# Encoder trunk in fp32 on one core: output projection reordered by row tiles, two-pass norm, and layer 2's token low parts from PSUM

## The chip, the core and the metric

One core of a Trainium2 chip runs the whole program. Times are device microseconds from the first to the last instruction of the core, as the runs give them. Engines: TensorE (PE, with its weight loads PEld), VectorE (DVE), ScalarE (ACT), GpSimd (POOL), SyncE (SP), which issues all the DMAs.

## What is computed

Two encoder layers over x (1, 1024, 1024), with D_MODEL = 1024 and D_INNER = 2048. Layer i does

```python
q, k, v, mq, gate = split_proj(einsum('bld,de->ble', x, w_in[i]), SPLIT)
o_mix = mixer_a(...) if i == 0 else mixer_b(...)     # windowed / dilated attention, 12 heads
o_mem = memory_attention(mq, mem, w_mkv[i])          # 4 heads
y = concat([o_mix, o_mem]) * silu(gate)              # (1024, 2048)
branch = einsum('ble,ed->bld', y, w_out[i])          # 2048 -> 1024
x = layer_norm(ALPHA * x + branch, ln_g[i], ln_b[i])
```

Everything is fp32. Below, *the first layer* is layer 0 of the code and *the second layer* its layer 1.

## The kernel before

**Products in three parts.** TensorE multiplies fp32r operands. Each fp32 operand is split in two, by ScalarE (`split_hi`, `columns_hi`, `y_tile`: a copy that rounds to fp32r, the high part) and VectorE (`split_lo`, `columns_lo`: the source less the high part, the low part). A product is three matmuls: high by high, high by low, low by high. Weights come by DMA in pieces of 128x512 (256 KB) into `raw` (6 slots), and are split into `ring` (4 slots, each a high and a low part); `AHEAD = 3` is how many pieces ahead the splits are issued.

**Input projection (`run`).** Each layer is a row of *pairs* of 128-column blocks (20 in the first layer, 40 in the second). A pair is computed from 7 products of 4 steps of 3 matmuls each (a Strassen-like scheme, 84 matmuls of 512 columns), with 7 operands made of the tokens, `xs[j]`, j = 0 to 6. Operand j is a half of the rows, or a sum or difference of halves (`token_sums` and its sisters, VectorE). Its rows have tokens on the partitions, and TensorE transposes them, four 128x128 blocks to a *group* (`x_group`, `rows_to_columns`, line 1063), into one of the four banks XB; ScalarE's copy (line 1306) takes the high part and VectorE's subtraction (lines 1581, 1536) the low part. There are 28 groups to a layer. `X_BEFORE` says ahead of which product of the first pair TensorE transposes which operands; in the second layer it is operand 0 before product 0, operands 1 and 2 before product 1, 3 before 2, 4 before 3, and 5 and 6 before product 4. The attention of earlier pairs is interleaved with the steps.

**Output projection (`out_projection`).** y comes back from DRAM in tiles of 128x512 (`y_raw`, two slots) and is split too (`y_split`, two slots). For each half h of the tokens and each block e of the 16 of D_INNER, TensorE adds 24 matmuls into all eight PSUM banks (4 token tiles by 2 column halves; `add_to`, lines 1256, 1260, 1262). All eight banks of a half end in its last two blocks (`last_two`). So the sums of the rows come at the end of a half, nearly together:

```python
for h in range(2):
    for e in range(NE - 2):
        is_split(h, e)
        for b in range(8):
            add_to(h, e, b, first=e == 0, ends=b >= 6)
    last_two(h)
```

VectorE then adds the residual (`add`, line 1878), and takes mean and variance (`statistics`, lines 1886 and 1889). GpSimd makes the standard deviation's inverse (`norms`: add epsilon, power -1/2, for tiles 4 to 7 two more for the bias). Rows 0 to 3 are normalised beside the second half's matmuls: VectorE subtracts the mean and multiplies (line 1896), multiplies by g, and GpSimd adds b over 128x1024 (line 1044). For rows 4 to 7, ScalarE normalises (line 1521), and VectorE multiplies by g and adds b (lines 1901 and 1904), each a `scalar_tensor_tensor` over 128x1024 by the helper `two`, line 1536. Its loop for the norms stands after the adds and statistics of all four tiles, so all the norms follow the last statistics.

**Order.** Each engine runs its own list; they meet in semaphores. SP's list holds the loads of weights (`loads_after`, released by `w_lo`), of y, the residual rows, g and b, the stores of y, and, after all the loads of the projection, the stores of the normalised rows (lines 997 and 1000). In the second layer TensorE takes operand 0 from rows 0 to 3 as soon as banks 4 to 7 are free; ScalarE reaches those groups after its four norms; VectorE reaches operand 0's low parts after its eight multiplications and additions. The first pair's `first_part` on ScalarE waits for all eight rows (lines 1324, 1325), because it writes into the same buffer.

## Time and profile before

| | |
|---|---|
| runs | 2168.25, 2169.8, 2172.13 us; median 2169.8 |
| profiled execution | 2170.46 us, of which the span is 2168.6 us |
| TensorE busy | 2107.2 us, 97% |
| VectorE busy | 1628.4 us, 75% |
| ScalarE busy | 1091.1 us, 50% |
| mean granted clock | 0.990 |

A row of the timeline gives the start and the time from the first start to the last end of one or more instructions. Matmuls overlap: one of 512 columns is listed with 0.39 us, but in a run of them a new one begins every 0.227 us at the full clock. The granted clock is 1.00 for 2.4 GHz and 0.50 for 1.2 GHz. "issue" is time in which the engine waited for nothing that the profile shows.

### The profile page before, as it was taken

How to read it: one execution, taken by the hardware profiler on the slowest of the kernel's cores; microseconds unless marked ns; L12 is line 12 of the kernel's file. 1: busy time of each engine (PE TensorE's matmuls, PEld its weight loads, DVE VectorE, ACT ScalarE, POOL GpSimd, SP SyncE). 2: the span in 40 equal slices, each digit the busy share in tenths (PEclk: the TensorE clock that was granted, in tenths of full speed). 3: DMA queues.
4: the chain of work that ended last, by engine and by line, in shares of the span. 5: the costliest groups of instructions: out<-in, count | busy, mean ns of one | idle time of the engine just before them, and what ended most of it. 6: DMA issues, size and time to landing. Idle time of an engine off the chain costs nothing.

```text
span 2168.6 us, 31853 instructions
## 1 busy us (share of the span) xinstructions
PE 2107.2 (97%) x10880; PEld 1767.9 (82%) x10880; DVE 1628.4 (75%) x3673; ACT 1091.1 (50%) x2649; POOL 48.4 (2%) x65
## 2 busy tenths in 40 slices
PE   8999999999999995999999999999999999999996
PEld 8888888888888774888888888888888888888875
DVE  6777878787663568868888888888887888775485
ACT  5444444445553323455555555555555565564332
POOL 0000000000000021000000000000000000000031
PEclk9999999999999997999999999999999999999998
DMA  8311111111126542123233133133143233224643
GB/s 266 103 48 42 60 39 49 59 59 59 54 80 216 182 141 102 54 69 94 63 97 93 56 100 95 50 108 99 50 108 86 63 108 85 89 87 161 216 142 131
DMA packets 244619, 209.20 MB, mean 96 GB/s; under 512 B 21092, under 2 KB 198316, under 8 KB 244460
## 3 DMA queue, kind: packets, MB, share of 16 engines
q1 hardware_dynamic: 244460, 207.16, 31.8%
q8 instruction: 89, 1.46, 0.3%
q14 instruction: 70, 0.57, 0.1%
HBM read 172.60 MB, written 34.52 MB: 96 GB/s over the span
## 4 chain that ended last, share of the span: by engine, by line
PE 78%; DVE 13%; DMA 5%; issue 2%; ACT 2%; SPq 0%; DVEq 0%; ACTq 0%
PE bank L1086 15%; PE bank L1084 15%; PE bank L1085 15%; PE bank L1162 8%; PE bank L1134 7%; DVE work L1536 5%; PE bank L1256 4%; PE bank L1260 4%; PE bank L1262 4%; PE bank L1148 4%; DVE ring L1536 2%; DMA work<-weight_scratch 1%; DMA weight_scratch<-trig 1%; DVE x_ops L1536 1%; PE bank L1063 1%
## 5 line engine op out<-in xcount | busy, mean ns | idle before, releaser
L1084 PE MATMUL bank<-x_ops,ring 128*128 128x512 f32 (+1 forms) x1808 | 844.5, 467 | 16.9 <-issue 14.8
L1086 PE MATMUL bank<-x_ops,ring 128*128 128x512 f32 (+1 forms) x1808 | 698.9, 387 | 0.0
L1085 PE MATMUL bank<-x_ops,ring 128*128 128x512 f32 (+1 forms) x1808 | 697.0, 386 | 0.0
L1536 DVE SCALAR_TENSOR_TENSOR ring<-raw,ring 128x512 fp32r<-128x512 f32 x400 | 272.9, 684 | 232.9 <-ACT ring L1302 232.6
L1086 PEld LDWEIGHTS bank<-x_ops,ring 128*128 128x128 f32 x1808 | 341.0, 189 | 71.3
L1084 PEld LDWEIGHTS bank<-x_ops,ring 128*128 128x128 f32 x1808 | 345.7, 191 | 61.4 <-issue 15.5
L1363 ACT COPY work<-bank 128x256 f32<-128x256 f32 (+2 forms) x448 | 164.3, 367 | 430.1 <-PE bank L1148 429.3
L1085 PEld LDWEIGHTS bank<-x_ops,ring 128*128 128x128 f32 x1808 | 345.5, 191 | 37.5
L1302 ACT CAST ring<-raw 128x512 fp32r<-128x512 f32 x400 | 246.5, 618 | 198.4 <-PE bank L1262 173.0
L1162 PEld LDWEIGHTS bank<-work 128*128 128x128 f32 x1744 | 262.2, 190 | 44.4 <-ACT work L1363 3.9
L1380 ACT ACTIVATE work<-work,soft 128x256 f32<-128x256 f32 (+2 forms) x448 | 226.5, 506 | 134.3 <-DVE soft L1680 132.6
L1134 PE MATMUL bank<-work 128*128 128x256 f32 (+2 forms) x896 | 267.2, 380 | 3.0 <-DVE soft L1680 3.0
L1162 PE MATMUL bank<-work 128*128 128x128 f32 x1744 | 267.6, 275 | 2.5 <-ACT work L1363 1.2
L1536 DVE SCALAR_TENSOR_TENSOR work<-work 128x512 f32<-128x512 f32 (+4 forms) x352 | 233.3, 678 | 34.5 <-DMA work<-weight_scratch 31.5
L1134 PEld LDWEIGHTS bank<-work 128*128 128x128 f32 x896 | 183.3, 215 | 39.9 <-DVE soft L1680 7.8
L1536 DVE SCALAR_TENSOR_TENSOR work<-work,trig 32x512 f32<-32x512 f32 x304 | 207.2, 710 | 0.8
L1256 PE MATMUL bank<-ring,x_ops 128*128 128x512 f32 x512 | 200.4, 391 | 6.9 <-DVE x_ops L1536 5.3
L1262 PE MATMUL bank<-ring,x_ops 128*128 128x512 f32 x512 | 199.3, 389 | 0.0
L1260 PE MATMUL bank<-ring,x_ops 128*128 128x512 f32 x512 | 199.3, 389 | 0.0
L1536 DVE SCALAR_TENSOR_TENSOR ring<-sums,ring 128x512 fp32r<-128x512 f32 x180 | 123.0, 683 | 68.2 <-ACT ring L1302 68.1
L1148 PE MATMUL bank<-ident,work 128*128 128x128 f32 x872 | 168.7, 273 | 0.5 <-DVE work L1690 0.5
L1148 PEld LDWEIGHTS bank<-ident,work 128*128 128x128 f32 x872 | 114.2, 140 | 34.9 <-ACT work L1380 4.5
(74 smaller groups left out, 2020.8 us busy)
## 6 DMA issues: line engine op xcount, KB each, us to landing
raw<-in_w_in_b SPq DMA_DIRECT2D x160, 256.0 KB, 3.1
raw<-in_w_out SPq DMA_DIRECT2D x128, 256.0 KB, 2.9
raw<-in_w_in_a SPq DMA_DIRECT2D x80, 256.0 KB, 3.0
work<-weight_scratch SPq DMA_DIRECT2D x24, 768.0 KB, 5.2
y_scratch<-work SPq DMA_DIRECT2D x32, 512.0 KB, 2.8
x_ops<-y_scratch SPq DMA_DIRECT2D x64, 256.0 KB, 3.7
work<-v_scratch SPq DMA_DIRECT2D x48, 256.0 KB, 4.4
raw<-in_w_mkv SPq DMA_DIRECT2D x32, 256.0 KB, 5.1
```

The source lines that it names most:

```text
L1084: nc.tensor.matmul(dst, w_h, x_h, start=start, stop=False, skip_group_check=again)
L1085: nc.tensor.matmul(dst, w_h, x_l, start=False, stop=False, skip_group_check=again)
L1086: return nc.tensor.matmul(dst, w_l, x_h, start=False, stop=stop, skip_group_check=again)
L1134: nc.tensor.matmul(SB[count % 2][:, 0:size], q, k, start=True, stop=True).then_inc(s_ready, 1)
L1148: mm = nc.tensor.transpose(TB[x_n % 2][:, c * P:(c + 1) * P], p[:, k0:k0 + P], ident[:, :])
L1162: mm = nc.tensor.matmul(dst, job.values(v), pT[layer][count % 2][:, c * P:(c + 1) * P], start=(c == 0), stop=(c == len(chunks) - 1))
L1256: mm = nc.tensor.matmul(BB[b][:, :], y_h, ring[:, n % RING, 0, :], start=first, stop=False)
L1260: nc.tensor.matmul(BB[b][:, :], y_h, ring[:, n % RING, 1, :], start=False, stop=False)
L1262: mm = nc.tensor.matmul(BB[b][:, :], y_l, ring[:, n % RING, 0, :], start=False, stop=last)
L1302: nc.scalar.copy(ring[:, n % RING, 0, :], src).then_inc(w_hi, 1)
L1380: nc.scalar.activation(p_view(layer, count % 3, size, sink), s_view(layer, count % 3, size, sink), ACT.Exp, bias=low[:, job.stat, t:t + 1] ...
L1536: return nc.vector.scalar_tensor_tensor(out=dst, in0=a, scalar=1.0, in1=b, op0=ALU.mult, op1=op)
```

## The change

**Output projection.** The 16 blocks fall into twelve early ones and four late ones (8 to 11). In each half, TensorE does the early blocks over all eight banks as before, and then, for one bank after the other, the four late blocks: 12 matmuls to a bank, so that a token tile is done every 24 matmuls. The late blocks' split weights are kept for both halves (`late`, 8 places in the region of operands 4 and 5, split once a layer, in the first half); their split y has four places of its own. So a layer's projection has 56 weight pieces and not 64. `y_raw` gets four slots. `AHEAD` is 3 as before, but the calls count single pieces.

**Norm.** VectorE adds epsilon; GpSimd's share is the power alone. VectorE does (x - mean) * g in one `scalar_tensor_tensor` (`scale`) and (that * rstd) + b in another (`shift`), both over 128x1024; for every tile of the second half both follow the tile's own statistics. ScalarE's norm, GpSimd's additions of b and VectorE's separate passes go. In the second layer the last tile is shifted and stored in two halves of the columns.

**Second layer's operands.** Operand 0's groups and their low parts are done within the first layer's output projection, three groups after token tile 6 (the third of the second half), one after tile 7. For operands 0 to 5 the low part is made in PSUM: a matmul of minus the unit matrix by the high part is added to the transposed group (`less_high`), and ScalarE copies the rest (`x_low`). Operand 5 moves to product 1, so that twelve groups (5, 1, 2) precede it. VectorE keeps the low parts of operand 6 alone. The token sums of the first kinds move from the second layer's beginning into the norm loop.

```diff
-OUT_STAGES = 4 * NE
+EARLY = (0, 1, 2, 3, 4, 5, 6, 7, 12, 13, 14, 15)
+LATE = (8, 9, 10, 11)
...
-RAW, RING, AHEAD = 6, 4, 3
+RAW, RING, AHEAD, Y_RAW = 6, 4, 3, 4
...
-                    ((0,), (1, 2), (3,), (4,), (5, 6), (), ()))
+                    ((), (5, 1, 2), (3,), (4,), (6,), (), ()))
...
+            def deviations(layer):
+
+                for t in range(TILES):
+                    pool.wait_ge(ln_eps, layer * TILES + t + 1)
+                    nc.gpsimd.tensor_tensor(rstd[:, t:t + 1], mv[:, t, 1:2], power[:, 0:1],
+                                            ALU.pow).then_inc(ln_rstd, 1)
...
+            def less_high(j, i):
+
+                number = x_number(1, j, i)
+                pe.wait_ge(xt_hi, number + 1)
+                nc.tensor.matmul(x_bank(number)[:, :].rearrange("p (k n) -> p k n", k=4), minus,
+                                 xs[:, j, 0, :, i * P:(i + 1) * P], start=False, stop=True,
+                                 skip_group_check=True).then_inc(xt_less, 1)
...
-                    if j == 0 and layer == 1:
-                        pe.wait_ge(z_free, 16)
+                    if j < 2 and layer == 1:
+                        pe.wait_ge(z_free, 8 + BRANCH_BANKS.index(j) + 1)
...
                 for h in range(2):
-                    for e in range(NE - 2):
+                    for e in EARLY:
                         is_split(h, e)
                         for b in range(8):
-                            add_to(h, e, b, first=e == 0, ends=b >= 6)
-                    last_two(h)
+                            add_to(h, e, b, first=e == EARLY[0], ends=b >= 6)
+                    for t in range(4):
+                        for c in range(2):
+                            for e in LATE:
+                                if t == 0 and c == 0:
+                                    is_split(h, e)
+                                add_to(h, e, 2 * t + c, last=e == LATE[-1])
+                        if layer == 0 and h == 1 and t >= 2:
+                            for i in ((0, 1, 2), (3,))[t - 2]:
+                                x_group(1, 0, i)
+                            for i in ((0, 1), (2, 3))[t - 2]:
+                                less_high(0, i)
...
+            def x_low(j, i):
+                number = x_number(1, j, i)
+                act.wait_ge(xt_less, number - 4 - X_GROUPS + 1)
+                nc.scalar.copy(xs[:, j, 1, :, i * P:(i + 1) * P],
+                               x_bank(number)[:, :].rearrange("p (k n) -> p k n", k=4)
+                               ).then_inc(xt_rest, 1)
...
+                second = 2 * NE + AHEAD
+                for m in range(AHEAD, second):
+                    stage(m)
+                for t in range(4):
+                    add(0, 2 * t)
+                    add(0, 2 * t + 1)
+                    statistics(t)
+                for m in range(second, OUT_STAGES + AHEAD):
+                    stage(m)
+                    t, step = divmod(m - second - 8, 2)
+                    if 0 <= t < 4:
+                        if step == 0:
+                            scale(t)
+                        else:
+                            shift(t, slice(0, D), ln_done)
+                if layer == 0:
                     third_sum(FIRST_PAIR[1])
                     fourth_sum(FIRST_PAIR[1])
                 for t in range(4, TILES):
-                    norm(t)
+                    add(1, 2 * (t - 4))
+                    add(1, 2 * (t - 4) + 1)
+                    statistics(t)
+                    if layer == 0 and t > 4:
+                        token_sums(1, t - 5)
+                        second_token_sums(1, t - 5)
+                    scale(t)
+                    if layer == 1 and t == 7:
+                        for half in HALVES:
+                            shift(t, half, ln_done_v)
+                    else:
+                        shift(t, slice(0, D), ln_done_v)
+                if layer == 0:
+                    token_sums(1, 3)
+                    second_token_sums(1, 3)
```

In `run(1)`, TensorE and ScalarE take the groups of a product one behind the other: group n is transposed (its high part copied), then `less_high` (and `x_low`) of group n - 1.

## Rows read from the trace of the kernel before

**Rows 1.** The page: busy time of each engine, and the chain by engine.
```profile
PE 2107.2 (97%) x10880; PEld 1767.9 (82%) x10880; DVE 1628.4 (75%) x3673; ACT 1091.1 (50%) x2649; POOL 48.4 (2%) x65
...
PE 78%; DVE 13%; DMA 5%; issue 2%; ACT 2%; SPq 0%; DVEq 0%; ACTq 0%
```

**Rows 2.** Busy time, granted clock and DMA by stretch; columns in line one.
```profile
core 0: us, PE busy (x) PEld busy (x) DVE busy (x) ACT busy (x) POOL busy (x), PEclk, DMA share, GB/s
...
646.40:736.00 89.60, 87.98 (x387) 72.48 (x388) 37.42 (x57) 29.98 (x50) 0.00 (x0) 1.00 0.64 209
736.00:825.70 89.70, 87.90 (x383) 71.06 (x381) 56.98 (x77) 27.55 (x46) 16.64 (x12) 1.00 0.49 159
825.70:849.00 23.30, 3.65 (x16) 2.70 (x16) 22.92 (x34) 7.93 (x10) 6.52 (x16) 0.58 0.22 90
849.00:854.00 5.00, 4.97 (x13) 3.89 (x14) 4.86 (x8) 0.00 (x0) 0.00 (x0) 0.55 0.00 0
854.00:861.00 7.00, 4.23 (x32) 3.49 (x31) 7.00 (x13) 4.31 (x9) 0.00 (x0) 0.95 0.00 0
...
870.00:887.00 17.00, 16.82 (x97) 14.07 (x96) 14.39 (x25) 9.14 (x18) 0.00 (x0) 1.00 0.12 32
```

**Rows 3.** Timeline of TensorE between the layers and through pair 20.
```profile
825.27 0.39 PE L1262 MATMUL bank<-ring,x_ops 128*128 128x512 f32 x1
...
849.03 0.76 PE L1084 MATMUL bank<-x_ops,ring 128*128 128x512 f32 x1 [14.82 <-issue]
...
874.18 1.91 PE L1063 MATMUL bank<-ident,work 128*128 128x128 f32 x16
...
886.48 0.39 PE L1086 MATMUL bank<-x_ops,ring 128*128 128x512 f32 x1
```

**Rows 4.** Timeline of VectorE between the layers.
```profile
832.38 1.24 DVE L1878 SCALAR_TENSOR_TENSOR work<-work,bank 128x512 f32<-128x512 f32 x2
833.66 1.29 DVE L1886 BATCH_NORM_STATS2 work<-work 128x6 f32<-128x512 f32 x2
834.98 0.21 DVE L1889 BATCH_NORM_AGGREGATE work<-work 128x2 f32<-128x12 f32 x1
...
836.86 9.67 DVE L1536 SCALAR_TENSOR_TENSOR work<-work 128x1024 f32<-128x1024 f32 x8
846.46 2.48 DVE L1536 SCALAR_TENSOR_TENSOR x_ops<-bank,x_ops 128x512 fp32r<-128x512 f32 x4
```

**Rows 5.** Timeline of TensorE at the end: its last matmul.
```profile
2150.66 0.39 PE L1262 MATMUL bank<-ring,x_ops 128*128 128x512 f32 x1
```

**Rows 6.** Timeline of VectorE at the end: its last group.
```profile
2155.98 9.62 DVE L1536 SCALAR_TENSOR_TENSOR work<-work 128x1024 f32<-128x1024 f32 x8
```

**Rows 7.** Waits of TensorE, 646 to 826 us: us in total, times, longest.
```profile
PE bank L1256 <- DVE x_ops L1536: 3.3, 5, 1.6
```

**Rows 8.** Waits of TensorE, 2063 to 2151 us: the same columns.
```profile
PE bank L1256 <- DVE x_ops L1536: 1.7, 4, 0.9
```

**Rows 9.** Timeline around 784 us: start us, us, engine, line, operation.
```profile
783.82 2.77 POOL L1044 TENSOR_TENSOR work<-work 128x1024 f32<-128x1024 f32 x1 [3.24 <-DVE work L1536]
...
784.26 2.88 DVE L1536 SCALAR_TENSOR_TENSOR x_ops<-x_ops 128x512 fp32r<-128x512 f32 x1
```

**Rows 10.** Timeline of ScalarE: copies of transposed columns in PSUM.
```profile
874.82 4.50 ACT L1306 CAST x_ops<-bank 128x512 fp32r<-128x512 f32 x8 [1.88 <-PE bank L1063]
```

**Rows 11.** Timeline of GpSimd: the power -1/2, VectorE light and busy.
```profile
2148.25 0.55 POOL L1032 TENSOR_TENSOR work<-work,power 128x1 f32<-128x1 f32 x1
...
2157.29 1.54 POOL L1032 TENSOR_TENSOR work<-work,power 128x1 f32<-128x1 f32 x1
```

**Rows 12.** DMA queue and issues, 646 to 736 us (KB each, us to landing).
```profile
GB/s 124 242 312 236 255 11 249 94 147 203 32 254 272 245 238 223 267 213 247 276 201 261 203 258 279 203 303 180 230 297 214 233 264 263 306 267 113 0 45 72
...
raw<-in_w_out SPq DMA_DIRECT2D x31, 256.0 KB, 3.1
x_ops<-y_scratch SPq DMA_DIRECT2D x16, 256.0 KB, 4.4
```

More of the change, by code:

```diff
@@ L60 @@
 MKV_STAGES = 4 * DEPTH * MEM_HEADS
-OUT_STAGES = 4 * NE
+EARLY = (0, 1, 2, 3, 4, 5, 6, 7, 12, 13, 14, 15)
+LATE = (8, 9, 10, 11)
+OUT_ORDER = []
+for half in range(2):
+    for place, block in enumerate(EARLY):
+        OUT_ORDER += [(half, block, 0), (half, block, 1)]
+        if half == 0 and place % 3 == 1:
+            OUT_ORDER += [(0, LATE[place // 3], 0), (0, LATE[place // 3], 1)]
+OUT_STAGES = len(OUT_ORDER)
+Y_ORDER = [(half, block) for half in range(2) for place, early in enumerate(EARLY)
+           for block in ((early, LATE[place // 3]) if place % 3 == 1 else (early,))]
 LAYER_STAGE = (MKV_STAGES, MKV_STAGES + PRODUCTS * PAIRS[0] + OUT_STAGES)
@@ L341, in encoder @@
         weight_in = sem("weight_in")
-        y_full = [sem("y_full0"), sem("y_full1")]
+        y_full = [sem(f"y_full{b}") for b in range(Y_RAW)]
         y_hi = sem("y_hi")
@@ new lines, in load_norm @@
+            def load_norm(layer, place):
+                row, src = ((g_row, ln_g), (b_row, ln_b))[place]
+                nc.sync.dma_start(row, src[layer].partition_broadcast(P)).then_inc(gb_in, 16)
+                if layer == 0 and place == 1:
+                    for m, src in ((m_b, mask_b), (m_w, mask_w), (m_b2, mask_b2)):
+                        nc.sync.dma_start(m, src).then_inc(mask_in, 16)
+            def out_projection(layer, residual, dst):
+                for m in range(AHEAD, OUT_STAGES + AHEAD):
+                    loads_after(OUT_STAGE[layer] + m)
+                    if m >= OUT_STAGES:
+                        continue
+                    h, e, c = OUT_ORDER[m]
+                    if c == 1 and e in EARLY:
+                        place = EARLY.index(e)
+                        if h == 0 and 5 <= place < 9:
+                            load_residual(layer, residual, place - 5)
+                        if h == 0 and place >= 10:
+                            load_norm(layer, place - 10)
+                        if h == 1 and 1 <= place < 5:
+                            load_residual(layer, residual, 3 + place)
+                    for q in y_events(m):
+                        if q + Y_RAW - 1 < 2 * NE:
+                            load_y(layer, q + Y_RAW - 1)
@@ L1182, in run @@
                             if g == FIRST_PAIR[layer]:
-                                for op in X_BEFORE[layer][j]:
-                                    for i in range(4):
-                                        x_group(layer, op, i)
+                                groups = [(op, i) for op in X_BEFORE[layer][j] for i in range(4)]
+                                for n, group in enumerate(groups):
+                                    x_group(layer, *group)
+                                    if layer == 1 and j < 4 and n > 0:
+                                        less_high(*groups[n - 1])
+                                if layer == 1 and j < 4 and groups:
+                                    less_high(*groups[-1])
                             product_begins(g, j)
@@ L1455, in run @@
                     if T < STEPS and T % 4 == 0:
-                        for op in X_BEFORE[layer][T // 4]:
-                            for i in range(4):
-                                x_group(layer, op, i)
+                        groups = [(op, i) for op in X_BEFORE[layer][T // 4] for i in range(4)]
+                        for n, group in enumerate(groups):
+                            x_group(layer, *group)
+                            if layer == 1 and T < 16 and n > 0:
+                                x_low(*groups[n - 1])
+                        if layer == 1 and T < 16 and groups:
+                            x_low(*groups[-1])
                     if T in fills[layer]:
@@ L1786, in run @@
                     if T < STEPS and T % 4 == 0:
+                        for op in X_BEFORE[layer][T // 4] if layer == 0 or T == 16 else ():
+                            for i in range(4):
+                                x_group(layer, op, i)
                         if layer == 1 and T in (4, 8):
@@ new lines, in scale @@
+                def scale(t):
+                    n = layer * TILES + t
+                    dve.wait_ge(ln_aggr, n + 1)
+                    dve.wait_ge(gb_in, 32 * (layer + 1))
+                    nc.vector.scalar_tensor_tensor(out=rows[:, t, :], in0=rows[:, t, :],
+                                                   scalar=mv[:, t, 0:1], in1=g_row,
+                                                   op0=ALU.subtract, op1=ALU.mult
+                                                   ).then_inc(ln_scaled, 1)
@@ new lines, in shift @@
+                def shift(t, cols, done):
+                    n = layer * TILES + t
+                    dve.wait_ge(ln_scaled, n + 1)
+                    dve.wait_ge(ln_rstd, n + 1)
+                    nc.vector.scalar_tensor_tensor(out=rows[:, t, cols], in0=rows[:, t, cols],
+                                                   scalar=rstd[:, t:t + 1], in1=b_row[:, cols],
+                                                   op0=ALU.mult, op1=ALU.add).then_inc(done, 1)
+                second = 2 * NE + AHEAD
```

341 lines of the change are left out of this document (144 added, 197 removed).

## The prediction

> **What bounds the kernel now.** I read the page first, for who is busy and who ends the chain: TensorE is busy 97% of the span and holds 78% of the chain, VectorE 13% [rows 1]. So only the places where TensorE stands still can give anything. The busy time by stretch shows where they are [rows 2]: both halves of the first layer's output projection are nearly full, and then come 23.3 us in which TensorE works for 3.65 us and VectorE for 22.92. The timeline gives the edges [rows 3]: the last matmul of the projection is issued at 825.27 and is through its slot at 825.5; the second layer's first product begins at 849.03; its first pair (pair 20) ends with the matmul of 886.48, at 886.7. That is 61.2 us for 84 matmuls that need 19.0 at 0.227 each. In between stands VectorE's list [rows 4]: per token tile two additions, two statistics and one aggregate (2.72 us from tile to tile), then eight passes of 1.2 us over 128x1024 (836.86 to 846.5), and only then operand 0's low parts (846.46, four of them), which release the product at 849.03. The end of the program has the same shape: last matmul at 2150.66, so done with its slot at 2150.9 [rows 5], VectorE's eight passes until 2165.6 [rows 6], last store landed at 2168.6, 3.0 us later. Last, TensorE's waits in the projections: 3.3 us [rows 7] and 1.7 us [rows 8] for the low parts of y. They have a cause: beside a 2.77 us addition of b on GpSimd, VectorE's low part of y takes 2.88 us, where its neighbours take 0.69 [rows 9].
>
> **Part 1, the projection.** It keeps 768 matmuls a layer; the order by tile changes their sequence, not their number. Twelve of them in a row into one bank is what the products of a pair do already, so I price that at nothing. GpSimd's four long additions a layer go, and with them the 5.0 us of waits [rows 7, 8]. What takes their place on VectorE, in the second half's early blocks, is per block two weight splits, one y split (0.6 each) and two passes of 1.2: 4.2 us, 4.8 in a block that also splits a late y, under the 5.44 us of its 24 matmuls. In the first half the late pieces make VectorE's and ScalarE's work per early block four thirds of before, about 2.4 us; that is covered as well. Between the halves VectorE's adds and statistics now come tile by tile; after the last bank it has about 2.7 us of them and 1.3 us of splits before the second block of the new half is needed, 5.44 us later: 1.4 us of cover, nothing charged. GpSimd's small operations and SP's order cost nothing: residual rows are asked for some 20 us ahead or more, the y tiles three ahead. **Gain 5.0 us**; bounds 0 (if other waits come) and 6.
>
> **Part 2, between the layers.** Time is counted from the last projection matmul, P.
> - Inserted before P: twelve transposes (16 take 1.91 us [rows 3], so 1.4) and two minus products of 0.23 with a short wait: 2.0 us on TensorE, which move no other thing.
> - After P: one group, its high copy, the last minus products, the last low copies by ScalarE (0.56 us each, from eight in 4.50 [rows 10]): 2.4 us. Product 0, 12 matmuls: 2.7. So it ends at P+5.1, where it now begins only at P+23.5 [rows 3].
> - ScalarE's first copy out of product 0 waits for the last tile's `shift`. VectorE works tile by tile: 2.72 for adds and statistics, 0.15 for epsilon (the aggregate takes 0.21 [rows 4]), 1.2 scale, some 0.35 waiting for GpSimd, 1.2 shift, and 1.2 of token sums: 6.8 us a tile against 5.44 plus the inserted groups. After P the last tile needs about 0.6 (latency, second addition) + 1.5 + 0.15 + 1.2 of token sums + 1.2 + 1.2: P+6.0. The copy of 0.7 ends at P+6.7. It is TensorE's queue behind `less_high` that waits, since the groups of product 1 stand ahead of product 1.
> - The twelve groups of product 1 need 24 copies on ScalarE, where now it makes one per group and VectorE the other side by side. 24 x 0.56 = 13.5 us if TensorE keeps its clock. TensorE then has per group 0.43 of transposes and 0.23 of product in 1.12 us. In the trace, the stretch of 7 us with only transposes and a gap behind product 0 ends at the lower level (0.95 over 854 to 861 [rows 2], and 0.58 in the gap before, where TensorE stood), while 4.3 us of transposes behind product 3 do not (1.00 over 870 to 887). A stretch of 13 us is nearer to the first. So I take the lower clock from about 4 us after product 0: ten groups at 4 x 0.213 + 0.43 = 1.3 us, 1.8 more than ScalarE's pace, plus what is in flight: the groups end at P+22.5. Product 1 then runs mostly at 1.2 GHz as 849 to 854 does (0.55 [rows 2]): 4.9 us and not 2.7: P+27.4.
> - Products 2 and 3: each is preceded by a copy of 0.7 and eight copies, 4.5 us, then 2.7: 7.9 each, P+43.2. VectorE did half of those copies before; now it is free there, which is worth nothing.
> - Operand 6 (1.9, VectorE makes the low part) and products 4 to 6 (8.2): P+53.3.
> In all 53.3 + 2.0 = 55.3 against 61.2: **gain 5.9 us**. With the full clock throughout it is 48.8 + 2.0, a gain of 10.4. The lower bound: the clock falls again in the groups of products 2, 3 and 4 (rival 2), a loss of 2.
>
> The cost of a minus product is not in the trace. Between nothing (hidden under the copies) and a whole slot at the low clock, 24 x 0.43 = 10 us, I take what the copies leave, because ScalarE's pace is the longer one.
>
> **Part 3, the end.** Now 2168.6 - 2150.9 = 17.7 us. After: VectorE needs 2.72 + 0.15 + 1.2 + 0.35 + 1.2 = 5.6 us a tile against TensorE's 5.44, so it is 0.6 late at the last tile and 0.2 behind by the matmul's latency. Then the second addition 0.65, statistics 1.5, epsilon 0.15, scale 1.2, waiting for the power 0.35, two half shifts 1.2, and the half tile's store: 2.9, from the 256 KB loads at 3.1 [rows 12] and today's 3.0 for 512 KB. Sum 8.7: **gain 9.0 us**. Bounds 7 and 10.5. The power takes 0.55 us on GpSimd with VectorE light and 1.54 beside the 128x1024 passes [rows 11]; 0.35 is what 1.54 leaves beyond the 1.2 of scale. The Trainium skill, "SBUF — State Buffer", "SBUF: two separate sides", says that a VectorE operation with two SBUF inputs and a GpSimd operation that reads SBUF exclude each other for a whole instruction. By that rule the power begins only when scale is over, each wait is some 0.65, and VectorE falls 1.2 us further behind at the end; the doubled times of [rows 9] agree with it.
>
> **Sum.** 5.0 + 5.9 + 9.0 = 19.9 us off the profiled execution of 2170.46 gives 2150.6. The median of the runs is 0.7 below that execution; so 2150.
>
> **Rivals.**
> 1. *The clock stays up* between the layers, because the gaps between pieces of work are under a microsecond. For: 4.3 us of transposes at 1.00 [rows 2]. Against: 13 us are three times that. 2170.5 - 5.0 - 10.4 - 9.0 = 2146.1, by the median 2145.
> 2. *The clock comes back for moments only.* Transposes don't keep it up, so it falls in the groups of products 2, 3 and 4 as well, since only 2.7 us of product lie between them. Each of two stretches costs 4 x 0.18 more for its groups and 2.4 for its product, 3.1; operand 6 and product 4 cost 1.7: 7.9 in all, 2158. Against it: 1.00 over 870 to 887 with two such stretches. The Trainium skill, "TensorE: Matmul & The Clock Gate", "PE-mode transpose", says that transposes don't count as busy in the way matmuls do. By that rule this rival is the case; the full clock behind 4 us of transposes [rows 2] neither proves nor refutes it.
> 3. *The chain of a group is serial*: high copy, minus product, low copy with the semaphores between, 1.5 us and not 1.12, because ScalarE's list alternates and finds the product unready. 20 groups x 0.38 = 7.6 later than with full clock or 5 later than forecast: 2155 to 2160.
> 4. *Slower: the loads bind the early blocks of the first half.* All 32 weight pieces, 16 y tiles, 4 residual rows, g and b, 16 MB, must now come in 65 us: 246 GB/s, where the trace shows 209 over the stretch at 0.64 share [rows 2]. If they came at 200, the early blocks would take 80 us, 14.7 more in each layer, 29.4 together: 2150 + 29 = 2179. It decides from about 217 GB/s downwards (10 us a layer eats the gain). Against it: single slices run at 250 to 312 GB/s [rows 12], pieces land in 3.1 and 4.4 us with six and three in flight, and 0.64 of the share for 209 leaves room for 320.
> 5. *The change does less than it says*: the pipeline by tile holds, but VectorE's order (token sums ahead of scale) delays the last shift by more than counted. It only moves ScalarE's gate, some 2 us: within the range.
>
> **How the numbers follow.** The forecast gets 0.45, rival 1 gets 0.25, rival 2 gets 0.13, rival 3 gets 0.08, rival 4 gets 0.04; 0.05 stays for a better outcome than all, a lower price of tail and gate together. The range goes from 2142 (rival 1 with the better ends of parts 1 and 3) to 2160 (rivals 2 and 3). A measurement of this kernel can tell about 0.2%, 4.3 us, from no change. Faster by more than that: all but rival 4 and a little of 2 and 3 with part 1 at its bound of nothing: 0.93. Within it 0.03, slower 0.04.
>
> **What would show it.** Waits of TensorE for low parts of y near zero in both projections; a gap under 3 us between the last projection matmul and product 0; TensorE at 60 to 80% with ScalarE at its copies in the next 15 us, and the granted clock there (0.5 or 1.00 tells the forecast from rival 1); pair 20 over some 53 us after P; VectorE one tile behind TensorE at the end, and the last store landing 8 to 9 us after the last matmul. I am wrong if TensorE waits for splits in the early blocks of a first half, if VectorE is more than a tile late, or if the twelve groups take over 18 us.

## The result, and the profile after

The changed kernel takes 2141.39 us (median of 4 runs, 2140.49 to 2143.5) against 2169.03 (4 runs, 2168.05 to 2172.13): ratio 0.9872, 95% interval 0.9854 to 0.9889. The forecast was 2150 (2142 to 2160): the direction was right, the size was not: 27.6 us were gained where the forecast had some 20. A second measurement (F1) gave 2143.4 us, ratio 0.9868 (0.9854 to 0.9882). The profiled execution has a span of 2138.7 us.

The page of the changed kernel, the rows that answer to [rows 1], and TensorE's costliest groups:

```profile
PE 2108.1 (99%) x10904; PEld 1771.9 (83%) x10904; DVE 1592.9 (74%) x3650; ACT 1078.2 (50%) x2650; POOL 16.6 (1%) x23
...
PE 85%; DVE 6%; DMA 3%; ACT 2%; issue 2%; SPq 1%; POOL 0%; DVEq 0%; POOLq 0%; ACTq 0%
...
L1157 PE MATMUL bank<-x_ops,ring 128*128 128x512 f32 (+1 forms) x1808 | 842.8, 466 | 2.8 <-DVE ring L1622 2.1
...
L1331 PE MATMUL bank<-ring,x_ops 128*128 128x512 f32 x384 | 149.6, 390 | 1.5 <-issue 1.5
```

TensorE's busy time is the same within 1 us; its share of the chain rises from 78% to 85%, VectorE's falls from 13% to 6%. `add_to` over the early blocks (the last row) waits for VectorE nowhere.

Where the time came from is best read by milestones of TensorE, in us from one to the next. They are worked out from the timelines of the two kernels (a matmul's slot of 0.227 is added to the last of a stage):

| stage | before | after | gain | forecast |
|---|---|---|---|---|
| start to the first projection | 646.45 | 645.88 | 0.6 | 0 |
| first projection, without the inserted 2.0 us | 179.05 | 174.35 | 4.7 | 3.3 |
| inserted groups and products | 0 | 2.0 | -2.0 | -2.0 |
| last projection matmul to product 0 | 23.5 | 2.5 | 21.0 | 21.1 |
| product 0 to the end of pair 20 | 37.7 | 45.0 | -7.3 | -13.2 |
| the other 39 pairs | 1086.2 | 1084.8 | 1.4 | 0 |
| second projection | 177.95 | 174.2 | 3.75 | 1.7 |
| last matmul to the end | 17.7 | 9.9 | 7.8 | 9.0 |

The sum is 29.9 us of span, where the forecast's terms sum to 19.9. "The other 39 pairs" took 1084.8 to 1092.0 us in the profiled executions of ten kernels that have the same code there, so 1.4 can't be put down to the change.

Busy time, granted clock and DMA by stretch, for [rows 2]:

```profile
core 0: us, PE busy (x) PEld busy (x) DVE busy (x) ACT busy (x) POOL busy (x), PEclk, DMA share, GB/s
646.40:729.00 82.60, 82.60 (x366) 68.38 (x365) 41.21 (x67) 29.11 (x51) 1.11 (x2) 1.00 0.64 208
729.00:822.25 93.25, 93.25 (x417) 77.06 (x416) 59.39 (x89) 24.46 (x43) 4.91 (x5) 1.00 0.44 150
...
827.60:831.10 3.50, 1.02 (x9) 0.78 (x7) 3.32 (x4) 1.15 (x4) 0.00 (x0) 0.98 0.12 48
831.10:834.70 3.60, 3.56 (x15) 3.01 (x15) 3.60 (x7) 2.73 (x6) 0.00 (x0) 0.55 0.26 101
834.70:842.90 8.20, 7.45 (x40) 4.90 (x38) 0.31 (x1) 8.20 (x17) 0.00 (x0) 1.00 0.00 0
842.90:858.00 15.10, 13.39 (x69) 10.18 (x68) 3.79 (x6) 11.25 (x23) 0.00 (x0) 1.00 0.18 53
```

Both projections are full. The clock did fall between the layers, but for less than 4 us (0.55 over 831.1 to 834.7), behind a stretch in which TensorE had worked 1.02 of 3.5 us. It came back within the groups, and stayed.

TensorE's timeline there, for [rows 3]. Line 1127 is the transposes, 1151 the minus product, 1331 to 1333 the projection, 1157 to 1159 the products of a pair:

```profile
822.02 0.39 PE L1333 MATMUL bank<-x_ops 128*128 128x512 f32 x1
...
824.75 0.47 PE L1157 MATMUL bank<-x_ops,ring 128*128 128x512 f32 x1 [0.72 <-issue]
...
827.58 1.03 PE L1127 MATMUL bank<-ident,work 128*128 128x128 f32 x8
831.14 0.80 PE L1151 MATMUL bank<-x_ops 128*128 128x512 f32 x1 [2.52 <-ACT x_ops L1376]
...
832.44 0.78 PE L1151 MATMUL bank<-x_ops 128*128 128x512 f32 x1
...
835.72 0.51 PE L1151 MATMUL bank<-x_ops 128*128 128x512 f32 x1
...
836.70 0.50 PE L1151 MATMUL bank<-x_ops 128*128 128x512 f32 x1
...
842.58 0.50 PE L1151 MATMUL bank<-x_ops 128*128 128x512 f32 x1 [0.48 <-ACT x_ops L1376]
842.92 0.40 PE L1157 MATMUL bank<-x_ops,ring 128*128 128x512 f32 x1
```

The last projection matmul begins at 822.02, product 0 at 824.75. Behind product 0 eight transposes go at once, then TensorE waits 2.52 us for ScalarE: that is the wait for the last `shift`. Groups at the lower clock come every 1.3 us (831.14, 832.44, then 833.72), the next after 1.03 (834.75), later ones every 0.98 (835.72 to 836.70 and on), and the last minus product waits 0.48 for its high copy. So the lower clock cost some 0.7 us here. Product 1 takes 2.8 us (842.92 to 845.71). ScalarE's side, for [rows 10]:

```profile
829.95 0.66 ACT L1392 ACTIVATE work<-bank 128x448 f32<-128x448 f32 x2 [4.78 <-DVE work L1989]
...
841.26 0.78 ACT L1385 CAST x_ops<-bank 128x512 fp32r<-128x512 f32 x1
841.74 0.79 ACT L1376 CAST x_ops<-bank 128x512 fp32r<-128x512 f32 x1
```

Its first copy begins at 829.95, 7.7 us after the last projection matmul, and from 835 on each copy takes its place every 0.48 us.

The end of the program, for [rows 5, 6, 11]: TensorE's last matmul, GpSimd's last power, and VectorE's last tile.

```profile
2128.57 0.39 PE L1333 MATMUL bank<-x_ops 128*128 128x512 f32 x1
```

```profile
2133.12 1.55 POOL L1107 TENSOR_TENSOR work<-work,power 128x1 f32<-128x1 f32 x1 [4.43 <-DVE work L1971]
```

```profile
2130.01 1.28 DVE L1957 SCALAR_TENSOR_TENSOR work<-work,bank 128x512 f32<-128x512 f32 x2
...
2132.98 1.28 DVE L1979 SCALAR_TENSOR_TENSOR work<-work 128x1024 f32<-128x1024 f32 x1
2134.78 1.42 DVE L1989 SCALAR_TENSOR_TENSOR work<-work 128x512 f32<-128x512 f32 x2 [0.52 <-POOL work L1107]
```

VectorE begins the last tile's first addition at 2130.01, when both banks are already full (2129.0), and so the second at 2130.65, 1.85 us after TensorE's last slot ends (2128.80). The forecast had 0.8. The power takes 1.55 us beside the scale, and VectorE waits 0.52 us for it before the shift. From VectorE's last instruction (2136.2) to the end (2138.7) the half tile's store takes 2.5 us.

The DMA of the first early blocks (mean rate, and issues with us to landing), for [rows 12]:

```profile
DMA packets 8348, 16.89 MB, mean 261 GB/s; under 512 B 930, under 2 KB 1314, under 8 KB 8343
...
raw<-in_w_out SPq DMA_DIRECT2D x31, 256.0 KB, 4.3
x_ops<-y_scratch SPq DMA_DIRECT2D x16, 256.0 KB, 5.1
```

261 GB/s over 64.6 us, with pieces landing in 4.3 and 5.1 us instead of 3.1 and 4.4. TensorE waited for none of them, so rival 4 was not the case.

### The profile page after: what moved, and what is told of

It is laid out like the page before. It is cut to its first block, busy times and chain, and to the rows that moved or that the text cites. A ratio compares the mean times of both kernels' runs of the same rounds, so it can differ in the third digit from the quotient of the medians.

```text
span 2138.7 us, 31823 instructions
## 1 busy us (share of the span) xinstructions
PE 2108.1 (99%) x10904; PEld 1771.9 (83%) x10904; DVE 1592.9 (74%) x3650; ACT 1078.2 (50%) x2650; POOL 16.6 (1%) x23
## 4 chain that ended last, share of the span: by engine, by line
PE 85%; DVE 6%; DMA 3%; ACT 2%; issue 2%; SPq 1%; POOL 0%; DVEq 0%; POOLq 0%; ACTq 0%
PE bank L1159 16%; PE bank L1157 16%; PE bank L1158 16%; PE bank L1235 8%; PE bank L1207 8%; PE bank L1331 5%; PE bank L1333 5%; PE bank L1332 5%; PE bank L1221 4%; DVE work L1622 2%; DMA work<-weight_scratch 1%; DMA weight_scratch<-trig 1%; DMA v_scratch<-work 1%; DVE ring L1622 1%; PE bank L1127 1%
## 5 line engine op out<-in xcount | busy, mean ns | idle before, releaser
L1622 DVE SCALAR_TENSOR_TENSOR ring<-raw,ring 128x512 fp32r<-128x512 f32 x368 | 251.5, 685 | 236.0 <-ACT ring L1372 235.8
L1372 ACT CAST ring<-raw 128x512 fp32r<-128x512 f32 x368 | 226.9, 618 | 166.8 <-PE bank L1333 147.0
L1622 DVE SCALAR_TENSOR_TENSOR work<-work 128x512 f32<-128x512 f32 (+3 forms) x328 | 204.9, 639 | 34.0 <-DMA work<-weight_scratch 31.4
L1331 PE MATMUL bank<-ring,x_ops 128*128 128x512 f32 x384 | 149.6, 390 | 1.5 <-issue 1.5
L1333 PE MATMUL bank<-ring,x_ops 128*128 128x512 f32 x384 | 149.5, 389 | 0.0
L1332 PE MATMUL bank<-ring,x_ops 128*128 128x512 f32 x384 | 149.5, 389 | 0.0
```

The lines of the kernel that those rows point to most:

```text
L1331: nc.tensor.matmul(BB[b][:, :], y[:, 0], w[:, 0, :], start=first, stop=False)
L1332: nc.tensor.matmul(BB[b][:, :], y[:, 0], w[:, 1, :], start=False, stop=False)
L1333: mm = nc.tensor.matmul(BB[b][:, :], y[:, 1], w[:, 0, :], start=False, stop=last)
L1372: nc.scalar.copy(split_slot(n)[:, 0, :], src).then_inc(w_hi, 1)
L1622: return nc.vector.scalar_tensor_tensor(out=dst, in0=a, scalar=1.0, in1=b, op0=ALU.mult, op1=op)
```

## The experiments

All are compared with the kernel before on the same chip. The milestones are those of the table above.

**E1: b on VectorE in the kernel before.**

```diff
-VECTOR_ROWS = 4
+VECTOR_ROWS = 8
...
-                    for t in range(4 * h, 4 * h + 4 - (VECTOR_ROWS if h == 1 else 0)):
+                    for t in range(0):
...
-                    act.wait_ge(ln_done, TILES - VECTOR_ROWS)
```

> The kernel before, with the additions of b for rows 0 to 3 moved from GpSimd to VectorE and nothing else. Theory (GpSimd's 2.8 us additions hold VectorE's low parts of y up): TensorE's waits for low parts of y in both projections go to under 0.5 us, the first layer's projection takes 175.5 to 176 us from its first to its last matmul instead of 179.05, the second's 174.5 to 175.5 instead of 177.95, and the whole comes to 2161 to 2163 us. Rival (the waits come from two y slots and the order of the last two blocks): the waits stay within 1 us of 5.0 and the time stays at 2169.

Measured: 2168.75 us (12 runs, 2164.48 to 2172.32) against 2170.92; ratio 0.9987 (0.9977 to 0.9996), which is 2.8 us. That is far from the 2161 to 2163 us of the theory. The first projection took 176.6 us, the second 175.7: 4.7 us of the 8.6 that both had lost against the 174.2 of a full one. In the first, what is left is mostly one wait where the halves meet:

```profile
PE bank L1256 <- DVE x_ops L1535: 1.7, 1, 1.7
```

So taking the additions off GpSimd gives back somewhat over half of the loss, although VectorE now makes them; I expected nearly all. The wait that is left is near 728, and in the kernel before it is there too (1.56 us): a y tile asked for at 721.25, behind b and the masks in SP's list, reaches ScalarE at 726.4. G1 takes that up. In the profiled execution the other pairs took 1092 us, the slowest of all, which hides the gain there; the runs as a whole show 2.8 of the 4.7 us, and where the rest went stays open.

**E2: low parts of operands 5, 1, 2, 3, 4 on VectorE.**

```diff
+        LESS = (0,)
...
-            first, last = 4 + X_GROUPS, 2 * X_GROUPS
+            first = 4 + X_GROUPS
+            last = first + 4 * len(LESS)
...
-                                    if layer == 1 and j < 4 and n > 0:
+                                    if layer == 1 and n > 0 and groups[n - 1][0] in LESS:
                                         less_high(*groups[n - 1])
...
-                        for op in X_BEFORE[layer][T // 4] if layer == 0 or T == 16 else ():
-                            for i in range(4):
+                        for op in X_BEFORE[layer][T // 4]:
+                            for i in range(4) if layer == 0 or op not in LESS else ():
                                 x_group(layer, op, i)
```

> The changed kernel with the minus product kept for operand 0 alone: for operands 5, 1, 2, 3 and 4 VectorE subtracts the high part from PSUM again (20 subtractions of 0.6 us) and ScalarE makes 20 copies fewer; order and places of the groups stay. Theory (ScalarE's 24 copies at 0.48 us set the pace of the twelve groups, VectorE is idle 9 us beside them): the groups before product 1 end about 3 us earlier, those before products 2 and 3 about 1.3 us earlier each, 2135 to 2137 us. Rival (the product in PSUM pays, because VectorE is late with the last norm and the token sums): the groups begin later by what VectorE still has to do, 2143 to 2146 us. For the clock: with transposes alone in those groups, if transposes do not hold the clock, it stays at 0.5 until product 1 and costs 3 us or more; if they do, it comes back within the groups as in the changed kernel.

Measured: 2135.66 us against 2170.92, ratio 0.9833 (0.9819 to 0.9847), 0.35% under the changed kernel's 0.9868 (F1, on another chip). Pair 20 ends 38.3 us after the last projection matmul, where the changed kernel has 47.5. The theory's sign is right and its size too small: 9.2 us earlier and not 5.6. TensorE's timeline (line 1129 the transposes, 1159 the first matmul of a product):

```profile
833.46 5.63 PE L1129 MATMUL bank<-ident,work 128*128 128x128 f32 x32 [3.86 <-DVE x_ops L1624]
...
838.85 0.48 PE L1159 MATMUL bank<-x_ops,ring 128*128 128x512 f32 x1
...
841.69 1.91 PE L1129 MATMUL bank<-ident,work 128*128 128x128 f32 x16
843.35 0.48 PE L1159 MATMUL bank<-x_ops,ring 128*128 128x512 f32 x1
```

The twelve groups are done and product 1 begins at 838.85, 16.5 us after the last projection matmul (20.7 in the changed kernel; the expectations of F2 have 16.8 for it, read from product 1's second matmul). Between the end of product 1 and product 2's first matmul lie only 1.66 us (841.69 to 843.35), against 4.4 in the changed kernel (845.71 to 850.07). That is what I had not counted. With transposes alone TensorE throws the four groups of operand 3 into four free banks and goes on, because product 2 does not need them. With the minus product it must wait in its own list for each high copy, before it may begin a product that needs none of them.

The clock in the same execution (columns as above):

```profile
833.00:834.00 1.00, 0.54 (x3) 0.57 (x4) 1.00 (x3) 0.00 (x0) 0.00 (x0) 0.64 0.00 0
...
836.00:838.00 2.00, 2.00 (x17) 1.89 (x16) 1.76 (x3) 1.60 (x5) 0.00 (x0) 0.82 0.00 0
838.00:840.00 2.00, 1.91 (x13) 1.52 (x12) 2.00 (x4) 1.94 (x5) 0.00 (x0) 1.00 0.00 0
```

TensorE stood still from 829.6 to 833.46, and the clock fell. It came back to 1.00 within the stretch 836 to 838, with nothing on TensorE but transposes since 833.46. So it came up beside transposes alone.

**E3: the first copy behind operand 5's groups.**

```diff
-                    if pair is not None:
+                    if pair is not None and pair.g != FIRST_PAIR[1]:
                         first_part(pair.g, 0, 0, r1_done)
...
+                            if layer == 1 and T == 4 and n == 4:
+                                first_part(FIRST_PAIR[1], 0, 0, r1_done)
                             x_group(layer, *group)
```

> The changed kernel with one item of ScalarE's list moved: the first copy out of the second layer's product 0, which waits for all eight normalised rows, comes behind the four groups of operand 5 instead of ahead of them. Theory (that wait alone keeps TensorE idle from 828.6 to 831.1 and makes the clock fall there): the idle 2.5 us becomes under 1 us, the granted clock stays at 1.00 through the groups, and the groups before product 1 end 2.5 to 3.5 us earlier: 2138 to 2139 us. Rival (the clock falls because transposes do not count as work): the clock falls to 0.5 within the groups all the same, some 4 us after product 0, and the gain is 2 us or less. Second rival: operand 1's groups then wait for the last token sums, and nothing is gained, 2141.

Measured: 2140.88 us against 2170.92, ratio 0.9861 (0.9846 to 0.9876); the changed kernel's 0.9868 lies in this interval, so the times tell nothing, and the 2138 to 2139 us of the theory were not reached. The milestones tell more: pair 20 ends 44.8 us after the last projection matmul instead of 47.5, the gain of 2.7 that the theory expects. The clock:

```profile
827.60:830.00 2.40, 2.16 (x17) 1.73 (x15) 2.36 (x3) 1.29 (x3) 0.00 (x0) 1.00 0.00 0
...
833.00:834.00 1.00, 0.58 (x4) 0.51 (x5) 1.00 (x3) 1.00 (x3) 0.00 (x0) 1.00 0.00 0
...
838.00:840.00 2.00, 1.72 (x9) 0.85 (x7) 0.00 (x0) 2.00 (x6) 0.00 (x0) 1.00 0.00 0
```

1.00 all through. Over 12.6 us TensorE had only transposes and minus products, with waits of up to 0.6 us, and kept its clock. Both rivals are refuted: the clock did not fall within the groups, and 2.7 us were gained.

**E4: in the second layer, norms behind all statistics.**

```diff
+                if layer == 1:
+                    for t in range(4, TILES):
+                        add(1, 2 * (t - 4))
+                        add(1, 2 * (t - 4) + 1)
+                        statistics(t)
                 for t in range(4, TILES):
-                    add(1, 2 * (t - 4))
-                    add(1, 2 * (t - 4) + 1)
-                    statistics(t)
+                    if layer == 0:
+                        add(1, 2 * (t - 4))
+                        add(1, 2 * (t - 4) + 1)
+                        statistics(t)
```

> The changed kernel, in the second layer's last half only: VectorE does the additions and statistics of all four tiles first and all scales and shifts behind them, as the kernel before did; the new two-pass norm and the blocks' order stay. Theory (the tile-by-tile order gives the gain at the end): from the last matmul to the last store 14.5 to 16 us instead of 9.9, the whole 2146 to 2147.5 us. Rival (it is the engine work saved by two passes, not their place): within 1.5 us of 2141.4.

Measured: 2147.56 us against 2170.92, ratio 0.9891 (0.9878 to 0.9905); from last matmul to end 15.4 us. VectorE at the end:

```profile
2130.01 0.69 DVE L1957 SCALAR_TENSOR_TENSOR work<-work,bank 128x512 f32<-128x512 f32 x1 [1.96 <-PE bank L1333]
...
2132.39 1.28 DVE L1979 SCALAR_TENSOR_TENSOR work<-work 128x1024 f32<-128x1024 f32 x1
...
2141.26 1.42 DVE L1989 SCALAR_TENSOR_TENSOR work<-work 128x512 f32<-128x512 f32 x2
```

Its last statistics end at about 2132.4, and 10.3 us of passes follow, as the 9.62 of [rows 6]. Of the 7.8 us gained at the end, 5.5 are the tile-by-tile place of the norms; the rival, which allows 1.5 us, is refuted. The other 2.3 have no run of their own. By the rows, the passes begin 2.5 us after TensorE's last slot and not 5.1, because VectorE has only one tile's statistics left, the halved last store takes 2.5 and not 3.0, and the passes themselves take 0.7 longer.

**F1: the changed kernel again.**

> The changed kernel itself once more, for a comparison on one chip with the three below: 2141 us, ratio to the kernel before 0.986 to 0.988.

2143.4 us against 2171.43, ratio 0.9868 (0.9854 to 0.9882); milestones within 0.4 us of the first time but for the other pairs (0.9 more).

**F2: E2 with operand 5's minus products kept (`LESS = (0, 5)`), E3, and F3's edit.**

> The changed kernel with three edits: minus products for operands 0 and 5 alone, VectorE making the low parts of 1, 2, 3 and 4; the first copy out of product 0 behind operand 5's groups; in the second layer VectorE takes the next tile's first addition between a tile's epsilon and its scale, so that GpSimd's power runs beside it. Theory: operand 5's groups run while VectorE still norms (no idle 3.9 us as with the low parts all on VectorE), the groups before product 1 end at about 15.3 us after the last projection matmul (20.7 in the changed kernel, 16.8 with VectorE alone), pair 20 ends 36 to 37 us after it (47.5 and 38.3), the clock stays at 1.00, the tail is 9.2: 2129 to 2132 us on a chip where the kernel before takes 2169. Rival (VectorE is the bound there either way, since the last token sums and third sums stand ahead of its low parts): pair 20 ends 38 us after it, 2133 us.

Measured: 2131.17 us against 2171.43, ratio 0.9811 (0.9796 to 0.9826). It beats the changed kernel of the same chip (0.9868) beyond both intervals, and is the fastest version here. Pair 20 ends 35.95 us after the last projection matmul, the tail (last matmul to end) is 8.8. The groups are done 14.2 us after the last projection matmul, where the theory has 15.3. VectorE:

```profile
828.77 1.28 DVE L1993 SCALAR_TENSOR_TENSOR work<-work 128x1024 f32<-128x1024 f32 x1
...
833.20 0.69 DVE L1626 SCALAR_TENSOR_TENSOR x_ops<-bank,x_ops 128x512 fp32r<-128x512 f32 x1 [0.41 <-ACT x_ops L1378]
834.18 4.28 DVE L1626 SCALAR_TENSOR_TENSOR x_ops<-bank,x_ops 128x512 fp32r<-128x512 f32 x7 [0.29 <-ACT x_ops L1378]
```

Its first low part (833.20) now waits for ScalarE's high copy and not the other way about; the clock read 1.00 in every stretch from 827 to 840. The theory holds; the rival, with its 38 us, does not.

**F3: the next tile's first addition between epsilon and scale.**

```diff
-                    add(1, 2 * (t - 4))
+                    if layer == 0 or t == 4:
+                        add(1, 2 * (t - 4))
                     add(1, 2 * (t - 4) + 1)
                     statistics(t)
+                    if layer == 1 and t < 7:
+                        add(1, 2 * (t - 3))
```

> The changed kernel with only the last of these edits. Theory (VectorE's two-operand pass shuts GpSimd's power out, and its wait of 0.52 us per tile puts VectorE 1.0 us behind TensorE by the last tile): the power takes 0.55 to 0.9 us beside the addition, no wait of VectorE for it but at the last tile, tail 9.2 us instead of 9.9. Rival (the power is slow beside any VectorE work): it takes 1.5 us again, VectorE's waits stay, tail 9.9.

One profiled run: the tail is 8.84 us instead of 9.92 (F1), and F2, which has the same edit, has 8.83. GpSimd:

```profile
2124.64 0.55 POOL L1107 TENSOR_TENSOR work<-work,power 128x1 f32<-128x1 f32 x1 [5.36 <-DVE work L1971]
2130.13 0.55 POOL L1107 TENSOR_TENSOR work<-work,power 128x1 f32<-128x1 f32 x1 [4.94 <-DVE work L1971]
2135.61 1.54 POOL L1107 TENSOR_TENSOR work<-work,power 128x1 f32<-128x1 f32 x1 [4.94 <-DVE work L1971]
```

The power takes 0.55 us beside the addition, which has one operand in PSUM, and 1.54 beside the last tile's scale, which has two in SBUF. The rival is refuted. The whole, 2142.95 us in one run, is too coarse to show 1 us.

**F4: E4's edit in the first layer.**

> The changed kernel, in the first layer's last half only: additions and statistics of all four tiles first, then token sums, scales and shifts of all. Theory (ScalarE's first copy, and with it the twelve groups, waits for the last shift): the last shift ends about 16 us after the last projection matmul instead of 7.6, the groups start that much later, the granted clock falls for longer, pair 20 ends 8 to 10 us later (56 us after the last matmul), 2150 us. Rival (the groups of operand 5, whose rows are ready, and the free ScalarE hide it): under 3 us later, 2144 us or less.

Measured: 2153.93 us against 2171.43, ratio 0.9917 (0.9903 to 0.993). The last shift ends 17.3 us after the last projection matmul (7.6 in the changed kernel), and pair 20 ends 57.4 us after it, 10.1 later than in F1. TensorE's wait for ScalarE's copy behind the last shift:

```profile
841.30 0.80 PE L1151 MATMUL bank<-x_ops 128*128 128x512 f32 x1 [12.23 <-ACT x_ops L1376]
```

The clock:

```profile
835.00:840.00 5.00, 0.00 (x0) 0.00 (x0) 4.82 (x5) 0.00 (x0) 0.00 (x0) 0.50 0.26 105
840.00:845.00 5.00, 3.70 (x14) 3.16 (x15) 4.85 (x9) 4.02 (x9) 0.00 (x0) 0.50 0.27 107
845.00:850.00 5.00, 4.82 (x29) 3.29 (x27) 0.17 (x1) 4.99 (x11) 0.00 (x0) 1.00 0.00 0
```

It fell while TensorE stood for 12.2 us and came back in the groups, at about 845. The theory holds; each of its sizes was somewhat small (16, 56 and 2150).

**G1: two raw slots for y instead of four.**

```diff
-RAW, RING, AHEAD, Y_RAW = 6, 4, 3, 4
+RAW, RING, AHEAD, Y_RAW = 6, 4, 3, 2
```

> The changed kernel with two raw slots for y instead of four, so that a y tile is asked for one ahead and not three; nothing else changes. Open is what caused the part of the projections' lost time that moving GpSimd's additions left (3.9 us of 8.6): in the kernel before, its largest wait (1.56 us, near 728) stands behind a y load issued at 721.25, after b and the masks, that lands 5 us later. Theory (y's loads are too short ahead): waits of TensorE for low parts of y come back in the first halves, most of all near the loads of g, b and the masks and at the late blocks' double y tiles; the first projection takes 2 to 8 us longer than 176.35, the second 1 to 5 us longer than 174.2, the whole 2145 to 2153 us. Rival (the order of the blocks and the freed VectorE list gave the rest): both projections within 0.5 us of the changed kernel, 2141 to 2143 us.

Measured: 2169.19 us (12 runs) against 2166.82, ratio 1.0012 (1.0003 to 1.0022). The sign is the theory's, the size far beyond it: the first projection takes 192.0 us instead of 176.35, the second 187.1 instead of 174.2, 28.6 us together, and the whole change is gone. Pair 20 (47.2) and the tail (9.9) stay as they were. Waits of TensorE from 640 to 840 us, and of ScalarE from 646 to 740:

```profile
PE bank L1331 <- DVE x_ops L1622: 9.9, 7, 2.2
```

```profile
ACT x_ops L1520 <- DMA x_ops<-y_scratch: 48.1, 12, 7.9
```

ScalarE stands 48.1 us for y tiles in the first half. With y tiles that take 5 us to land, two of them in every third block, and only one asked for ahead, the new order of blocks does not keep TensorE fed; it rests on the four slots. Between 0.6 and 0.8 of what TensorE loses shows in the list of its waits (9.9 of 15.7 us, 10.3 of 12.9). In the first projection the clock is part of the rest: behind waits of 1.85 and 1.80 us it fell twice, each time for 3.4 us (columns as above).

```profile
684.60:688.00 3.40, 3.40 (x10) 2.66 (x9) 0.72 (x2) 0.62 (x1) 0.00 (x0) 0.50 0.74 188
705.10:708.40 3.30, 3.30 (x9) 2.56 (x8) 0.25 (x1) 0.00 (x0) 0.00 (x0) 0.50 0.74 243
```

Matmuls are 0.43 us apart there and not 0.227, so this cost 3.1 us. Behind a wait of 2.18 us at 763.5 the clock stayed at 1.00.

## Why the prediction was wrong in size

**The clock between the layers** is the step that failed. I took the lower level for ten of the twelve groups (1.3 us each) and for product 1 (4.9 us), by the 7 us stretch of [rows 2] that ended low. That stretch held a gap of nearly 3 us without work; from E2 and E3 I infer that its fall goes with the gap, not with the transposes; no run closes that gap in the kernel before. E3 shows 12.6 us of transposes and minus products at 1.00, E2 a clock that comes back beside transposes alone. The fall in the changed kernel comes with the wait of 2.52 us for ScalarE, since it is gone in E3 with the wait. It lasted some 3.4 us and cost some 0.7: two groups at 1.3 us and one at 1.03 instead of 0.98, and product 1 took 2.8 us and not 4.9. Rival 1, a clock that stays up, came nearest: it put pair 20's end 48.8 us after the last projection matmul; 47.5 was measured, against 53.3 of the forecast. It had a chance of 0.25 and should have had the most. The Trainium skill ("TensorE: Matmul & The Clock Gate", "PE-mode transpose") says that the full clock does not engage for transposes, because they don't count as busy in the same way. E2 does not agree with it: there the clock came back to 1.00 between 836 and 838 with only transposes running. Rival 2 is refuted by the changed kernel's own clock, which is 1.00 over 842.9 to 858.0, the groups of products 2 and 3 included.

**ScalarE's copies** were priced at 0.56 us from a row of eight in 4.50 [rows 10]. Its last four copies come 0.6 apart, because they wait for transposes; its first three steps are 0.48. In the changed kernel they take 0.48: over 24 copies and twice eight, 3.2 us less. Rival 3, with 1.5 us a group, was not the case: the groups come every 0.98 us once the clock is back. ScalarE's first copy out of product 0, on the other hand, came 1.7 us later than forecast (7.7 us after the last projection matmul and not 6.0): VectorE was late at the last tile already, so that its second addition ended 2.0 us after that matmul and not 0.6. That is rival 5, within its 2 us.

**The waits in the projections** were read too low: 5.0 us from [rows 7, 8], 8.4 gained. [rows 8] begins in the middle of the second projection; over the whole of it the view lists 2.0 us in five waits, so 5.3 us in ten for both. The view counts from a matmul's listed end, 0.39 us after its start, though its slot is 0.227, and after the first matmul behind a wait (listed with 0.47) the next begins 0.31 us later. So each of the ten waits costs some 0.24 more than it is listed with, and the shortest don't appear. The length of the stage against that of a full one (179.05 and 177.95 against 174.2) gives the right number. In G1 20.2 us are listed and 28.6 lost, of which 3.1 are the clock.

**The cause of those waits** was half right: E1 gives back 4.7 of 8.6 us without GpSimd's additions. The rest includes y tiles that landed late; how much of it they are in the kernel before was not measured alone. I had named "the y tiles three ahead" as a reason to charge nothing, and did not see that this small edit carries the whole: by G1 it is worth 28.6 us under the new order, the clock's 3.1 included.

**Rival 4** named the right place, the first half's early blocks, and the wrong quantity. The rate was there (261 GB/s); by G1 it is how far ahead y is asked for that decides, and y alone was varied.

**The inserted groups** (2.0 us) and the gap before product 0 (2.5 against 2.4) came out as worked.

**The end**: 9.9 against 8.7. VectorE takes 5.97 us a tile (2124.03 to 2130.01) and not 5.6, against TensorE's 5.44, so that it begins the last tile's second addition 1.85 us after TensorE's last slot instead of 0.8. It waited 0.52 us per tile for the power instead of 0.35. The Trainium skill's rule of exclusion ("SBUF — State Buffer", "SBUF: two separate sides") gave waits of 0.65 and 1.2 us more in all, which is 9.9. The trace agrees with the rule: the power takes 1.55 us beside scale and ends 0.41 after it, and 0.55 in F3 beside the addition out of PSUM. That the sum comes out to the tenth is partly luck, since the last store took 2.5 us and not 2.9.

**What the change does badly** I did not foresee. Low parts through PSUM were put down as free because VectorE's time was idle. In fact they cost 9.2 us between products (E2): twice the copies on ScalarE, and a TensorE that waits in order for copies that its next product doesn't need. The change gains in spite of them, by the place of the norms (10.1 us between the layers by F4, 5.5 at the end by E4), and by full projections.

In the profiled executions the gain is 10.0 us above the forecast: 5.8 from the last projection matmul to pair 20's end, 3.4 in the projections, 2.0 at the start and in the other pairs, which is not the change's doing, and 1.2 less at the end. The medians are 7.8 above it (27.6 against 19.8).

The range missed by 0.6 us at its lower end. That end was rival 1 with the better ends of parts 1 and 3; part 1's was 6 us where 8.4 were gained, and with those it would have held.

Not tried: four y slots in the kernel before, with its own order of blocks; so how the last 3.9 us of its waits divide stays open. Nor was the blocks' order run without the rest of the change.

## What to carry to other kernels

Where all accumulators end together, the engine behind TensorE starts its whole chain at once: ordering the last blocks by accumulator lets it work tile by tile, and the tile-by-tile norms were worth some 15 us at two places (F4, E4). A denser order needs its transfers asked for earlier, each kind for itself: count what lies between a load's release and its use, not the mean rate. Moving work to an idle engine is not free if an in-order engine must then wait for the handshake; ask what stands behind the wait in its list, and whether it needs the result. Lost time is a stage's length less its instructions' slots, not the sum of its waits; look at the clock for the rest.

## What was not expected of the hardware

Transposes held TensorE's granted clock at 1.00 (E3, 12.6 us with minus products between), and it came back from 0.50 to 1.00 beside transposes alone (E2, between 836 and 838, where they had run since 833.46). A pause of 2.5 us behind a little work went with its fall in the changed kernel (1.02 us busy in 3.5), waits of 1.85 and 1.80 us did so in G1, and one of 2.18 us in G1 did not. GpSimd's power over 128x1 takes 0.55 us beside a VectorE operation with one operand in PSUM and 1.54 beside one with two in SBUF (F3). Two raw slots for y instead of four cost 28.6 us (G1), 3.1 of them by the lower clock.
